# Hybrid decoder layer on one core: five small reorderings in the mLSTM heads and at the start of the sample group's block selection

## The reference

```python
# mLSTM, for each head h of 4
qk   = (q @ k.T) * exp(dmat - m)                 # decayed scores, causal
num  = qk @ v + sc * (C @ q)                     # C: the sample's matrix state
hc   = num / max(|den|, exp(-m))
C_new = sl * C + sum(wl * v k^T);  n_new = sl * n + sum(wl * k)
out  = (rmsnorm(hc) + skip * uc) * sigmoid(o)    # the gate: o is moT below

# sparse attention of the samples
kc, vc  = compress(past keys), compress(past values)     # blocks of 32
p       = softmax(q kc); o_cmp = p vc; imp = sum over group of p
idx     = top_k(priority(imp), 16)                       # blocks of 64
o_sel   = softmax(q k[idx]) v[idx];  o_win = softmax(q k_window) v_window
o_nsa   = g0 * o_cmp + g1 * o_sel + g2 * o_win
```

## Time and profile before

| what | before |
|---|---|
| median of 3 runs | 1076.31 us (1075.5 to 1076.8) |
| the profiled execution's own time | 1076.65 us |
| its span | 1074.9 us |
| PE busy | 1018.1 us (95%) |
| DVE busy | 612.9 us (57%) |
| ACT busy | 404.1 us (38%) |
| POOL busy | 152.7 us (14%) |
| mean granted clock of PE | 0.985 |

### The profile page before, as it was taken

One profiled execution on the slowest core, in us unless ns is written; L12 is line 12 of the kernel. 1 busy time (PEld: TensorE's weight loads), 2 busy tenths in 40 slices (PEclk: granted clock), 3 DMA queues, 4 the chain that ended last, 5 costly groups with the idle time before them and its releaser, 6 DMA issues.

```text
span 1074.9 us, 19288 instructions
## 1 busy us (share of the span) xinstructions
PE 1018.1 (95%) x7776; PEld 917.0 (85%) x7776; DVE 612.9 (57%) x1305; ACT 404.1 (38%) x759; POOL 152.7 (14%) x207
## 2 busy tenths in 40 slices
PE   4999998999999979989899999999999999999996
PEld 4999998999866647665559999999999999999996
DVE  3736753444267656677957336676767677932222
ACT  4223422333143346448764333333333333621212
POOL 3200020330112221016740000000000000000000
PEclk9999999999999989999999999999999999999999
DMA  6561162553511165334012222222222222332322
GB/s 185 186 180 40 56 205 79 209 184 138 240 44 42 42 259 198 122 110 141 2 59 100 78 81 82 81 81 81 81 81 81 81 81 56 91 93 65 96 54 88
DMA packets 82074, 114.26 MB, mean 106 GB/s; under 512 B 10086, under 2 KB 72648, under 8 KB 79263
## 3 DMA queue, kind: packets, MB, share of 16 engines
q1 hardware_dynamic: 75247, 70.60, 21.2%
q0 software_dynamic: 6768, 42.84, 10.8%
HBM read 103.33 MB, written 13.59 MB: 109 GB/s over the span
## 4 chain that ended last, share of the span: by engine, by line
PE 83%; DVE 8%; DMA 3%; ACT 2%; issue 2%; POOL 1%; SPq 0%; DVEq 0%; ACTq 0%
PE banks L1619 14%; PE banks L1617 11%; PE banks L1659 6%; PE banks L1074 5%; PE banks L1129 5%; PE banks L1658 5%; PE banks L1077 4%; PE banks L1078 4%; PE banks L1572 3%; PE banks L1113 2%; PE banks L1571 2%; PE banks L1329 2%; PE banks L1318 2%; PE banks L1690 2%; PE banks L1393 1%
## 5 line engine op out<-in xcount | busy, mean ns | idle before, releaser
L1619 PE MATMUL banks<-xnT_r,RB_r 128*128 128x320 f32 x352 | 109.8, 312 | 0.0
L1619 PE MATMUL banks<-xnT_r,ring_r 128*128 128x320 f32 x352 | 109.4, 311 | 0.0
L1617 PE MATMUL banks<-xnT_r,RB_r 128*128 128x256 f32 x352 | 103.3, 294 | 0.0
L1617 PE MATMUL banks<-xnT_r,ring_r 128*128 128x256 f32 x352 | 98.9, 281 | 0.0
L1619 PE MATMUL banks<-RC_r,RB_r 128*128 128x320 f32 x264 | 82.3, 312 | 0.0
L1129 PE MATMUL banks<-RA,RB 128*128 128x128 f32 (+1 forms) x512 | 71.8, 282 | 2.9 <-DVE RA L1948 1.5
L1617 PE MATMUL banks<-RC_r,RB_r 128*128 128x256 f32 x264 | 74.3, 281 | 0.0
L2345 DVE TENSOR_TENSOR ring_r<-ring,RB_r 128x2048 fp32r<-128x2048 f32 x22 | 49.4, 2289 | 38.1 <-ACT RB_r L886 38.1
L1129 PEld LDWEIGHTS banks<-RA,RB 128*128 128x128 f32 x512 | 65.0, 191 | 4.4 <-ACT RA L668 2.3
L1617 PEld LDWEIGHTS banks<-xnT_r,RB_r 128*128 128x128 f32 x352 | 67.0, 190 | 1.2
L1617 PEld LDWEIGHTS banks<-xnT_r,ring_r 128*128 128x128 f32 x352 | 67.5, 192 | 0.0
(11 more groups left out here) (651 smaller groups left out, 2928.2 us busy)
## 6 DMA issues: line engine op xcount, KB each, us to landing
ring<-in_w_up_dram SPq DMA_DIRECT2D x22, 1024.0 KB
ring<-in_w_down_dram SPq DMA_DIRECT2D x8, 1408.0 KB, 7.0
ring<-in_w_in_dram SPq DMA_DIRECT2D x10, 1024.0 KB, 6.2
RB<-in_state_win_dram SPq DMA_DIRECT2D x8, 512.0 KB
out_win_s_dram<-in_state_win_dram POOLq DMA_DIRECT2D x1, 4032.0 KB
xsp<-RC SPq DMA_DIRECT2D x1, 2304.0 KB, 9.0
xT<-xsp SPq DMA_DIRECT2D x1, 2304.0 KB, 12.9
RA<-in_x_prompt_dram SPq DMA_DIRECT2D x4, 512.0 KB, 5.6
```

Source lines behind the costliest of these rows:

```text
L1617: t.matmul(ps[4 + par][:, w * UA:(w + 1) * UA], wk[:, w, k, c], x[:, 0:UA], skip_group_check=True, **first)
L1619: last = t.matmul(ps[2 * par + w][:, 0:UB], wk[:, w, k, c], x[:, UA:T], **on)
```

## The change

Five edits, and no arithmetic is added or left out.

1. ACT, first pass of the samples' attention: `keys(0, 2)` stands ahead of `exp_cmp(1)`, not behind it. Passes 1 to 3 keep their order.
2. The last head's output gate is a DVE instruction behind `mix_head(3)`; POOL's `gated(3)` is gone.
3. In each head, DVE makes `kbd` behind W, not ahead of `mix_head(h-1)` and W.
4. ACT counts `m_proja` behind the key columns and once more behind the key rows. PE waits for the first ahead of the score matmuls with j = 0 and 1, and for the second ahead of j = 2.
5. PE waits for `c_kcd` behind the four transposes of L1192, not ahead of them.

```diff
@@ POOL
-            gated(MH - 1)
             g.memset(Vbd, 0.0).then_inc(S("p_pool"), 1)
@@ ACT, projected_act
-                a.activation(mkT[:, 0:SEQ], ps[2][:, :], ACT.Copy, scale=KSCALE)
+                a.activation(mkT[:, 0:SEQ], ps[2][:, :], ACT.Copy, scale=KSCALE).then_inc(S("m_proja"), 1)
@@ ACT, the loop over passes
                 if p < 4:
                     keys(p, 1)
+                if p == 0:
+                    keys(p, 2)
                 if p < 3:
                     exp_cmp(p + 1)
-                if p < 4:
+                if 0 < p < 4:
                     keys(p, 2)
@@ PE, from compression to the heads
-            pe.wait_ge(S("c_kcd"), 2 + 2 * 8)
             pe.wait_ge(S("m_rcol"), 1)
             for k in range(MH):
                 last = t.transpose(ps[5][0:27, k * P:(k + 1) * P], mcg[:, k, :], ident[:])
             last.then_inc(S("m_cols"), 1)
 
+            pe.wait_ge(S("c_kcd"), 2 + 2 * 8)
             pe.wait_ge(S("pool_step"), 6)
@@ PE, heads
-                pe.wait_ge(S("m_proja"), h + 1)
+                pe.wait_ge(S("m_proja"), 2 * h + 1)
                 for j in range(4):
+                    if j == 2:
+                        pe.wait_ge(S("m_proja"), 2 * h + 2)
...
-            pe.wait_ge(S("m_proja"), MH + 1)
+            pe.wait_ge(S("m_proja"), 2 * MH + 1)
@@ DVE, mix_head
+                if h == MH - 1:
+                    dve.wait_ge(S("m_mixd"), MH)
+                    dve.wait_ge(S("m_mix"), MH - 1)
+                    v.tensor_tensor(xnT[:, h, :], xnT[:, h, :], moT[:, h, :], ALU.mult).then_inc(S("m_mix"), 1)
@@ DVE, heads
-                v.scalar_tensor_tensor(out=kbd[0:NSMP, :, :], in0=bmask.unsqueeze(2).to_broadcast([NSMP, NB, P]), scalar=0.0,
-                                       in1=mk[0:NSMP, 4:5, :].to_broadcast([NSMP, NB, P]), op0=ALU.is_equal,
-                                       op1=ALU.mult)
                 if h:
...
                                 ALU.mult).then_inc(S("m_w"), 1)
+                v.scalar_tensor_tensor(out=kbd[0:NSMP, :, :], in0=bmask.unsqueeze(2).to_broadcast([NSMP, NB, P]), scalar=0.0,
+                                       in1=mk[0:NSMP, 4:5, :].to_broadcast([NSMP, NB, P]), op0=ALU.is_equal,
+                                       op1=ALU.mult)
                 dve.wait_ge(S("m_p7"), 5 * h + 2)
```

## The result

The changed kernel took 1067.79 us (median of five runs, 1066.72 to 1070.52). The kernel before, run beside it, took 1076.80 (1075.5 to 1076.98). The ratio is 0.9926, 95% interval 0.9908 to 0.9944: 8.0 us less, 6.0 to 9.9. Applied to the 1076.31 of the forecast the ratio gives 1068.3, where 1070.7 was forecast: right in its sign, 2.4 us short in size, and on the very low end of the range. The profiled execution took 1070.52, its span is 1068.8.

The account below looks back on a forecast made before the run. PE was taken as the bound (83% of the chain), with gains only where it stands still. 0.53 + 0.29 + 0.50 + 0.83 + 3.47 = 5.62 us off the 1076.31 median gave 1070.7 us, range 1068.3 to 1073.3.

Parts of the forecast that it names:

- a wait of 0.3 in edit 5: Between compression and heads: DVE's last copy of compressed values would still be late next, by 0.3 us, before the gate rows.
- rival A: Head 2: the clock stays up there as well and falls nowhere else; 1.48 us more, 1069.2 us, chance 0.14.
- 0.9 for head 0 and the ACT chain: Low end of the range: 0.9 us for ends rounded down, in head 0 and the ACT chain.
- cover for `kbd`: Heads: DVE's 3.04 us idle before L2087 covers the 1.13 us delay behind W; without it, 1.13 a head, 4.5 in all.
- B: Pass 0 runs at half clock though the long wait is gone; gain 1.4 us instead of 3.47, 1072.8 us, chance 0.16.
- C: Pass 0: something else holds `score(0, 2)` or the next mask for 3 us; 2.15 us gain left, 1074.2 us, chance 0.05.
- The clock, weighed: Head 2 and pass 0: none of head 2's 1.48 us half-clock loss booked as gain; pass 0 taken at full clock.

Follow-up runs that it names:

- edit 1 alone: Kernel before with only the third key pair of pass 0 copied ahead of the second exponentials: 1074.72 us, ratio 0.9977.
- edits 2 to 5 alone: Four kernels, each the kernel before with one edit, in number order: 1076.78, 1074.39, 1077.52 and 1074.84 us.
- three last kernels: Changed kernel with `few_turned(0)` ahead of `score(0, 1)`: 1068.91 us; with half of `turn_kept` before head 3's W wait: 1068.57; both plus early ACT table load: 1067.12.
- edit 4 alone: Kernel before with only the split count of ACT's copies, PE waiting for two and later for the third: 1077.52 us, ratio 1.0007.
- filled wait in head 3: Changed kernel with 5 of the 10 `turn_kept` transposes done before PE's wait for W in head 3: 1068.57 us, ratio 0.9927.

## Why the prediction was right, and where it fell short

The mechanism was right in the five edits, but for a wait of 0.3 in edit 5 that isn't there, and the traces show it place by place. That the size came out inside the range is in part luck. Its low end was made of rival A, the clock in head 2, and of 0.9 for head 0 and the ACT chain, and none of these is shown to be what was missing.

- **Edit 5, 0.53 forecast, 0.73 measured.** The copy was booked as late next by 0.3. It isn't: the gate rows follow PE's own transposes by 0.2 at most, without a wait.
- **Edits 3 and 4, 1.62 forecast, 2.03 measured** (0.51, 0.53 and 0.99 in heads 1, 2 and 3, for 0.29, 0.50 and 0.83). The mechanism holds in each head: waits of 0.29 gone before the scores, none before the numerators of head 2, 1.30 in head 3 for the forecast 1.24. The reading that was short is that of the bracket: the trace shows 0.29 idle, and 0.5 is won. In head 3 the scores start 0.94 after the start of the transposes ahead of them before the change (361.94, 362.88), and 0.49 with it (360.07, 360.56): the wait of 0.29, and 0.16 by which PE's own instructions now overlap. The cover for `kbd` was there too: DVE's idle time before the copies of the numerators in head 3 falls from 4.27 to 3.13, by the 1.13 of `kbd`.
- **Edit 2, nothing forecast, nothing measured.** Its instruction takes 0.76 (0.75 forecast), and the landing ends 0.98 behind it.
- **Edit 1, 3.47 forecast, 3.44 measured**, by the predicted path: the copies in ACT's idle time, `score(0, 2)` 0.89 behind `score_few(1)`, DVE as the bound, PE idle 0.67 before `turn_sel(0, 0)` for the forecast 1. Rivals B and C are refuted by the traces: the clock stays up in pass 0, and the wait is gone. That edit 1 alone is worth 2.5 us in the runs rather than 3.5 is not explained. The account below would give it 2.9 to 3.8: 3.44, and 0.275 times what is left of its 4.7 us less at half clock behind the 3.4 or 6.8 of pass 0.
- **The term that was too small** is the clock. "The clock, weighed" ends its part on the heads with "I book none of these 1.48 us", and the sum has less half clock in pass 0 alone. At equal clock the sum is 6.20, not 5.62, which is 0.6 of the 2.4 that were missing. The rest goes with the clock, as far as a slope over runs can say. The runs of the changed kernel spend 26.0 us at half clock, those of before 39.8. Of these 13.8, the fall in pass 0 is 3.4 in three and 6.8 in five of the eight traces that have it, and it lies inside the 3.44 of edit 1. The other 7.0 to 10.4, at 0.275 each, make 1.9 to 2.9, and with 6.2 that is 8.1 to 9.1, for 8.0 by the ratio and 8.57 +- 0.5 by the means. The 0.275 is a slope over runs and not the price of one fall, so this last step is an estimate. Rival A had the right direction but one place: head 2. Both traces of the changed kernel are at full clock there, but the first has a fall in head 1 in its stead. Nor do the edits decide that place: the clock falls there in both traces of before, but in none of the four with one of edits 2 to 5 alone, the two without any gain among them. What changes is how long it is down over the whole kernel.
- The single edits agree with this: edits 1, 3 and 5 alone have 4.7, 5.3 and 4.0 us less at half clock than before (errors 1.5 to 1.9). They add up to 14.0, with an error near 3. For edit 1 the place is shown. For edits 3 and 5 it is not: their traces have five falls each up to pass 0, where those of before have four and six, and one trace each doesn't decide. And as the three last kernels have less waiting than the changed one and more time at half clock, why the changed kernel has so little stays open.
- A rival for part of the 1.8 us is untested. PE's wait for the state's transfer in head 2 is in no term of the prediction. It is 1.1 to 1.7 us in eight of the fourteen traces and absent in six (edits 2, 3 and 5 alone, and the last three kernels). Both traces of before and both of the changed kernel have it, so these don't differ by it, but how often the unprofiled runs of each kernel have it isn't known.
- The Trainium skill, "TensorE: Matmul & The Clock Gate", Part 1, ties the clock to the array's activity. The trace agrees where PE stands still for 3.43 us, and does not where the clock is 0.56 over a stretch in which PE is busy all the time (325.00 to 328.50). The forecast of pass 0 was by the part that holds.

## What to carry to other kernels

Read a wait together with what comes behind it: edit 4 alone and the filled wait in head 3 only handed their 0.3 and 0.6 us on to the next wait, while edit 4 paid once edit 3 had cleared the work ahead of W. Before pricing a half-clock stretch from one trace, get the mean granted clock of many runs: here a removed wait of 3.4 us took a fall with it in each of six traces, and other falls moved about and weighed as much as a whole edit. When a chain through ACT starves PE, look for copies that stand behind a wait they don't need. That one change of order was worth more than half of the traced sum, 3.44 of 6.20.

## What the runs showed of the hardware that was not expected

- The granted clock falls to half in a stretch with PE busy throughout. In the changed kernel's head 1 the 20 matmuls of L1274 take 4.14 rather than 2.50, right behind matmuls of 4 partitions (L1209 to L1212), with no wait since the 0.66 before 304.31. In eight of the fourteen traces a fall begins within 0.6 us behind the start of these matmuls in head 1. In the other six the place is at full clock, in the second trace of the same kernel too. What decides it is not shown.
- With the DMA engines at some 90% from loads of 512 KB, a 16 KB write landed 3.6 us after its issue. It was the same whether a gather of 2 MB started 0.7 us ahead of the landing or 0.3 us behind it.
